# A separate body for experts with up to 32 rows, on four column groups of TensorE

## What is computed

```python
logits = hf @ router_w + router_b                    # (256, 32)
top_val, top_idx = lax.top_k(logits, 4)
top_w = jax.nn.softmax(top_val, axis=-1)
...
def expert_block(args):                              # x of one expert's rows
    xb, e = args
    g = xb @ w_gate[e] + b_gate[e]                   # w_gate, w_up, w_down: (1024, 1024)
    u = xb @ w_up[e] + b_up[e]
    g = jnp.minimum(g, SWIGLU_LIMIT)
    u = jnp.clip(u, -SWIGLU_LIMIT, SWIGLU_LIMIT)
    act = g * jax.nn.sigmoid(SWIGLU_ALPHA * g) * (u + 1.0)
    return act @ w_down[e] + b_down[e]
...
y = y.at[row_tok].add(yb * row_w[:, None])
```

## Time and profile before

| | us |
|---|---|
| median of 3 runs | 2553.96 |
| lowest, highest | 2553.76, 2555.77 |
| span of the profiled execution | 2552.7 |
| expert stage in it, first gate matmul to the end of the last combination | 442.1 to 1437.7 |
| experts 12 and 13, up to up | 831.00 to 860.41 |

### The profile page before, as it was taken

One profiled execution on the slowest core, in us unless ns is written; L12 is line 12 of the kernel. 1 busy time (PEld: TensorE's weight loads), 2 busy tenths in 40 slices (PEclk: granted clock), 3 DMA queues, 4 the chain that ended last, 5 costly groups with the idle time before them and its releaser, 6 DMA issues.

```text
span 2552.7 us, 24185 instructions
## 1 busy us (share of the span) xinstructions
PE 2212.0 (87%) x9951; PEld 1237.3 (48%) x9952; DVE 651.7 (26%) x997; ACT 357.1 (14%) x548; POOL 103.9 (4%) x116
## 2 busy tenths in 40 slices
PE   6977789998899999999999797799979686858997
PEld 2643346333333333333333384488548475837873
DVE  2747623110111111111111115100016465420000
ACT  1211012111111111111111212100012221211000
POOL 1000010000000000000000100200000031200000
PEclk9888889999999999999999898899979887988999
DMA  9561155998699999969999741343333200013330
GB/s 346 207 230 50 66 192 204 398 428 359 263 427 428 427 428 428 428 262 413 428 427 417 290 163 65 83 151 146 133 130 132 99 1 1 1 67 116 139 109 17
DMA packets 106791, 580.77 MB, mean 228 GB/s; under 512 B 6992, under 2 KB 8084, under 8 KB 81969
## 3 DMA queue, kind: packets, MB, share of 16 engines
q1 hardware_dynamic: 101008, 562.40, 55.1%
q0 software_dynamic: 5696, 17.18, 2.2%
HBM read 578.49 MB, written 1.07 MB: 227 GB/s over the span
## 4 chain that ended last, share of the span: by engine, by line
PE 67%; DMA 16%; DVE 11%; ACT 3%; issue 2%; SPq 0%; DVEq 0%; POOL 0%; ACTq 0%
DMA ring<-in_w_up 14%; PE ps L1199 14%; PE ps L1586 12%; PE ps L1597 6%; PE ps L604 6%; PE ps L612 5%; PE ps L1214 5%; PE ps L516 1%; PE ps L1931 1%; PE ps L1222 1%; PE ps L1937 1%; DMA ring<-in_ada_w 1%; PE ps L825 1%; PE ps L1941 1%; PE ps L793 1%
## 5 line engine op out<-in xcount | busy, mean ns | idle before, releaser
L1199 PE MATMUL ps<-ring,arena 128*64 128x512 f32 x1632 | 362.6, 598 | 29.5 <-DMA ring<-in_w_up 23.5
L1586 PE MATMUL ps<-arena,ring 128*128 128x256 f32 x1408 | 308.2, 382 | 1.5 <-ACT arena L581 1.5
L1586 PEld LDWEIGHTS ps<-arena,ring 128*128 128x128 f32 x1408 | 270.0, 192 | 39.6 <-ACT arena L581 2.3
L1214 PE MATMUL ps<-ring,arena 128*64 128x512 f32 x1088 | 240.9, 594 | 9.0 <-ACT arena L1161 9.0
L1199 PEld LDWEIGHTS ps<-ring,arena 128*64 128x64 f32 x1632 | 114.7, 138 | 271.7 <-issue 231.2
L1134 DVE TENSOR_SCALAR arena<-ps 128x512 f32<-128x512 f32 x34 | 23.5, 692 | 546.3 <-PE ps L1199 546.3
L1214 PEld LDWEIGHTS ps<-ring,arena 128*64 128x64 f32 x1088 | 88.3, 137 | 139.1 <-issue 138.3
L1597 PE MATMUL ps<-ring,arena 128*128 128x512 f32 x352 | 151.4, 592 | 0.0
L604 PE MATMUL ps<-arena,ring 128*128 128x256 f32 x672 | 149.1, 384 | 0.7 <-ACT arena L581 0.7
L604 PEld LDWEIGHTS ps<-arena,ring 128*128 128x128 f32 x672 | 129.1, 193 | 20.4 <-issue 1.5
L1199 PE MATMUL ps<-arena 128*64 128x512 f32 x544 | 124.5, 611 | 11.2 <-issue 11.2
(11 more groups left out here) (453 smaller groups left out, 2147.5 us busy)
## 6 DMA issues: line engine op xcount, KB each, us to landing
ring<-in_w_up SPq DMA_DIRECT2D x64, 2048.0 KB, 17.3
ring<-in_w_down SPq DMA_DIRECT2D x64, 2048.0 KB, 16.2
ring<-in_w_gate SPq DMA_DIRECT2D x32, 2048.0 KB, 15.9
arena<-in_w_gate SPq DMA_DIRECT2D x32, 2048.0 KB, 15.9
ring<-in_ffn_w_gate_up SPq DMA_DIRECT2D x22, 2048.0 KB, 7.9
ring<-in_ada_w SPq DMA_DIRECT2D x12, 2048.0 KB, 17.7
ring<-in_ffn_w_down SPq DMA_DIRECT2D x10, 2048.0 KB, 7.7
ring<-in_w_in SPq DMA_DIRECT2D x8, 2048.0 KB, 18.0
```

The source lines that it names most:

```text
L1199: m = pe.matmul(bank(b)[c * CAP:(c + 1) * CAP, :], xT[:, j * P + h * CAP:j * P + (h + 1) * CAP], w[h][:, j, c * 512:(c + 1) * 512], start= ...
L1214: m = pe.matmul(bank(b)[d * CAP:(d + 1) * CAP, :], actT[:, j * P + h * CAP:j * P + (h + 1) * CAP], down_w[h][:, j, d * 512:(d + 1) * 512], ...
L1586: m = pe.matmul(bank(b0 + g)[:, c * SEQ:(c + 1) * SEQ], w[:, k, (2 * g + c) * P:(2 * g + c + 1) * P], hT2[:, k, :], start=(k == 0), stop=( ...
```

## The change

Experts with up to 32 rows (`FEW`) take a body of their own, `few`, which lies in the loop ahead of `narrow`; each engine now has two branches in a body. On PE:

- gate and up are one product. Each step of the contraction has four matmuls of 32 array columns: gate's two halves and up's two halves, side by side in one bank. 32 matmuls in 8 steps. It starts when both gate and up are there, and `g_ps` and `u_ps` are both raised by its last step. The biases are four more matmuls behind the first step.
- gather, transposes of gathered rows, weights and hidden values follow, in another order than before.
- down has four groups too: two halves of the output by two halves of the contraction, 16 matmuls in 4 steps. The two contraction halves stay on different rows of PSUM; the combination adds them, because its matrix now holds each weight twice.

For that, DVE's `dve_choose` makes the combination matrix in three instructions for each of the two token tiles instead of one (in the first round of every expert, whatever its body), with two tables, `far` and `both`, made once ahead of the loop. `pe_open` moves in the narrow, wide and further bodies from ahead of the combination of the expert before to the start of its own expert. In the bodies for over 128 rows a branch is dropped. SP's code is not touched.

```diff
+FEW = CAP // 2
...
+            o(dve.tensor_scalar(far, bank(7)[:, 2 * E:3 * E], float(FEW), float(2 * SEQ), ALU.is_gt, ALU.mult))
+            o(dve.tensor_scalar(both, posm, float(FEW), None, ALU.add))
+            o(dve.tensor_tensor(both[:, :, 0:E], both[:, :, 0:E], rows_bc(far, TT), ALU.add))
             o(dve.tensor_copy(cnt, bank(7)[:, 2 * E:3 * E]), pos_ready)
...
-                m = dve.tensor_scalar(Pw[:, t, :], slot_iota(r, 2 * CAP), posm[:, t, bass.ds(e, 1)], wt[:, t, bass.ds(e, 1)],
-                                      ALU.is_equal, ALU.mult)
+                if r == 0:
+                    dve.tensor_scalar(Pm, slot_iota(0, 2 * CAP), posm[:, t, bass.ds(e, 1)], None, ALU.is_equal)
+                    dve.drain()
+                    dve.scalar_tensor_tensor(Pm, slot_iota(0, 2 * CAP), both[:, t, bass.ds(e, 1)], Pm, ALU.is_equal, ALU.add)
+                    dve.drain()
+                    m = dve.tensor_scalar(Pw[:, t, :], Pm, wt[:, t, bass.ds(e, 1)], None, ALU.mult)
...
         def pe_narrow(pe, e, odd, there):
             n = e + 1
+            pe.wait_ge(main.pwT_ready, n)
+            pe_open(pe, 0, odd, 0)
+            pe_open(pe, 1, odd, 1)
             pe.wait_ge(main.x_ready, n * 2)
...
-            pe.wait_ge(main.pwT_ready, n + 1)
-            pe_open(pe, 0, 1 - odd, 0)
-            pe_open(pe, 1, 1 - odd, 1)
             pe_combine(pe, main, n, PwT[odd])
+
+        def pe_few(pe, e, odd, there):
+            n = e + 1
+            pe.wait_ge(main.pwT_ready, n)
+            pe.wait_ge(main.x_ready, n * 2)
+            there(0)
+            there(1)
+            for h in range(2):
+                for j in range(4):
+                    for i, (w, done) in enumerate(((gate_w[odd], main.g_ps), (up_w, main.u_ps))):
+                        for c in range(2):
+                            m = pe.matmul(bank(0)[(2 * i + c) * FEW:(2 * i + c + 1) * FEW, :],
+                                          XT[:, j * P + h * CAP:j * P + h * CAP + FEW], w[h][:, j, c * 512:(c + 1) * 512],
+                                          start=((h, j) == (0, 0)), stop=((h, j) == (1, 3)), tile_position=(0, (2 * i + c) * FEW), skip_group_check=True)
+                        if (h, j) == (1, 3):
+                            m.then_inc(done, 1)
+                    if (h, j) == (0, 0):
+                        for i in range(2):
+                            for c in range(2):
+                                pe.matmul(bank(0)[(2 * i + c) * FEW:(2 * i + c + 1) * FEW, :], Ee[odd][i * E:(i + 1) * E, 0:FEW],
+                                          bgu[i * E:(i + 1) * E, c * 512:(c + 1) * 512], start=False, stop=False,
+                                          tile_position=(i * E, (2 * i + c) * FEW), skip_group_check=True)
+            pe_gather(pe, main, n + 1)
+            pe_gatherT(pe, main, n * 2 + 1)
+            pe.wait_ge(main.a_ready, n * 2)
+            pe_weights(pe, main, n + 1)
+            for j in range(4):
+                m = pe.transpose(bank(0)[:, j * CAP:(j + 1) * CAP], every4(act_[0:CAP, :], j), ident[0:CAP, 0:CAP])
+            m.then_inc(main.aT_ps, 1)
+            there(2)
+            pe.wait_ge(main.aT_ready, n)
+            for j in range(4):
+                for d in range(2):
+                    for h in range(2):
+                        g = 2 * d + h
+                        m = pe.matmul(bank(2)[g * FEW:(g + 1) * FEW, :], actT[:, j * CAP + h * FEW:j * CAP + (h + 1) * FEW],
+                                      down_w[h][:, j, d * 512:(d + 1) * 512], start=(j == 0), stop=(j == 3), tile_position=(0, g * FEW))
+            m.then_inc(main.d_ps, 1)
+            pe_combine(pe, main, n, PwT[odd])
...
         def pe_wide(pe, e, odd, x, there):
+            pe.wait_ge(main.pwT_ready, n)
+            pe_open(pe, 0, odd, 0)
+            pe_open(pe, 1, odd, 1)
...
                     n_e = eng.value_load(cnt[0:1, bass.ds(e, 1)], min_val=0, max_val=SEQ)
+                    eng.br_cond(n_e > FEW, f"many_{which}{odd}", f"few_{which}{odd}")
+                    nc.switch_bb(f"few_{which}{odd}", parent=fork)
+                    few(i, e, odd)
+                    eng.br(f"next_{which}{odd}")
+                    nc.switch_bb(f"many_{which}{odd}", parent=fork)
                     eng.br_cond(n_e > CAP, f"large_{which}{odd}", f"small_{which}{odd}")
```

More of the change, by code:

```diff
@@ L987, in block_kernel @@
         mk = ar3(13792, 64, TT)
+        far, both = ar(21504, E), ar3(21536, TT * (E + 1), TT)
+        Pm = ar(21632, P)
         wt, posm = ar3(13856, TT * (E + 1), TT), ar3(13924, TT * (E + 1), TT)
@@ new lines, in act_few @@
+        def act_few(act, e, odd):
+            n = e + 1
+            act.wait_ge(main.gm_ready, n)
+            act.activation(sg[0:CAP, :], gm[0:CAP, :], ACT.Sigmoid, scale=ALPHA).then_inc(main.sg_ready, 1)
+            act_gathered(act, main, n * 2 + 1)
+            act_gatheredT(act, main, n * 2 + 2, XT)
+            act_weights(act, main, n + 1, PwT[1 - odd])
+            act.wait_ge(main.aT_ps, n)
+            act.copy(actT[:, 0:4 * CAP], bank(0)[:, 0:4 * CAP]).then_inc(main.aT_ready, 1)
+            act_out(act, main, (main.d_ps, n))
@@ new lines, in dve_few @@
+        def dve_few(dve, e, odd):
+            n = e + 1
+            dve.wait_ge(main.pwT_ps, n)
+            dve_choose(dve, main, e + 1, 0, 1 - odd)
+            dve.wait_ge(main.u_ps, n)
+            dve.tensor_scalar(gm[0:CAP, :], bank(0)[0:CAP, :], LIMIT, None, ALU.min).then_inc(main.gm_ready, 1)
+            dve.tensor_scalar(um[0:CAP, :], bank(0)[CAP:2 * CAP, :], LIMIT, -LIMIT, ALU.min, ALU.max).then_inc(main.a_ready, 1)
+            dve.drain()
+            dve.scalar_tensor_tensor(um[0:CAP, :], um[0:CAP, :], 1.0, gm[0:CAP, :], ALU.add, ALU.mult)
+            dve.drain()
+            dve.wait_ge(main.sg_ready, n)
+            dve.tensor_tensor(act_[0:CAP, :], um[0:CAP, :], sg[0:CAP, :], ALU.mult).then_inc(main.a_ready, 1)
@@ L1321, in pe_further @@
             pe.wait_ge(main.x_ready, e * 2 + 2)
+            pe.wait_ge(main.pwT_ready, e + 1)
+            pe_open(pe, 0, odd, 0)
+            pe_open(pe, 1, odd, 1)
             pe_gather(pe, extra, x)
@@ L1349, in dve_further, with expert_rounds @@
             dve_glu(dve, extra, x, (extra.g_ps, x), (extra.u_ps, x))
-        def expert_rounds(eng, narrow, wide, further):
+        def expert_rounds(eng, few, narrow, wide, further):
             which = eng.engine.name
```

22 lines of the change are left out of this document (9 added, 13 removed).

## The result

The changed kernel takes 2638.6 us (median of 4, 2636.3 to 2643.2) against 2554.9 of the kernel before on the same chip (2553.8 to 2561.8): 1.033 times, interval 1.031 to 1.035. A second comparison gave 2644.8 against 2553.3, 1.036 (1.033 to 1.038). The direction was forecast, the size was not: about 84 us instead of 38.5, and above the upper end of the range, 2612. The profiled execution has a span of 2634.3 us, 81.6 more than before, and all of it lies in the expert stage, which now ends at 1520.9 instead of 1437.7.

A forecast was written before the change was run, and what follows sets the result against it. The weight stream's transfers were taken to bound the kernel. Gaps +41.0, small terms +3.3, +0.5, -0.8, +0.6 and the stage's end -6.1 gave +38.5 us: 2592.5 us, main range 2575 to 2610, with (a) 2558 to 2612.

The forecast's parts named there:

- The slack of 7.9 us: Weight queue in the full stream: a gate transfer may be issued 7.9 us later before the stream gets a gap.
- The eleven places of the gaps: Few experts whose gap counts in full: 1, 2, 12, 13, 15, 17, 18, 24, 25, 28, 29; +41 us in all.
- The end: End of the expert stage: T + 42.6 us, T being when expert 30's up has landed, instead of 48.7 behind it.
- Up of expert 31: End of the stage: its second half lands at T + 23 us, T being when expert 30's up has landed.
- Part 2: Few experts' joined products: idle PE lowers the clock, adding 2.2 us (1.4 to 2.7), so each gap is 3.7 us.
- the 1.5: Stream delay per few expert at full clock, in us, from gate issued 9.45 us later against the slack of 7.9.
- Part 5: Moved openings, DVE's choice, extra branches: no cost in the stream; narrow bodies at 28.8 us, still under 29.4.
- rival (c): PE's doubled loop code must be fetched again in each body: some +60 us more, 2652 us; chance 0.06.
- Part 4: End of the expert stage, experts 30 and 31: shorter by 6.1 us.
- Rival (b): PE is the limit where the chain names it, so faster: 2505 us, or 2549 in a milder form; chance 0.08.
- (d): Column groups from different buffers don't overlap: joined product takes 14 us instead of 7, 2670 us; chance 0.03.
- (a): Gaps without the clock: it stays at 1.00, so +12 us, 2566 us; chance 0.14.

The follow-up runs named there:

- parted_nowide: Changed kernel with gate and up computed apart again, in two groups each, and the wide body never taken: 2491.6 us.
- warm_split: Changed kernel, wide body never taken, with 16 unread filling matmuls between the waits for gate and up and 8 behind the combination of few bodies: 2544.4 us.
- never_few: Changed kernel with the few bodies in the loop but never taken, experts up to 64 rows running the narrow body: 2599.6 us.
- no_few: Changed kernel with the few bodies' code and branch removed from the loop, openings at the start and DVE's longer choice kept: 2557.2 us.
- tail_joined: Kernel before's loop with DVE's longer choice, last pair of experts taken out and given the change's own few body: 2554.3 us, 1.000 times the kernel before.
- parted: Changed kernel with gate and up computed apart again, each in two groups of 32 columns, the rest of the few body kept: 2585.7 us.
- swapped: Few bodies in the loop but never taken, with the odd wide body ahead of the even one in memory: 2596.0 us.

## Why the prediction was wrong in size

**Right.** The kernel is bound by the stream of weights, and its price is the time of issue: confirmed by parted_nowide. The joined product costs what one product did, 8.2 us with its biases at full clock (experts 0 and 31). The slack of 7.9 us: with the gate issue found at T + 11.8 it gives 1.25 + 11.8 - 7.9 = 5.1 (5.15), and the five gaps from expert 12 to 20 are 4.9 to 5.8; with the issue of warm_split at T + 8.4 it gives 1.8, measured 2.0. The eleven places of the gaps, none behind narrow bodies. The end: 43.4 us instead of 42.6. Up of expert 31, T + 24.1 instead of T + 23.

**Part 2, the clock's term, mis-sized.** The gap was to be 1.5 + 2.2 = 3.7. Over the nine gaps in the stream (experts 12 to 29) it is 5.1 in the mean: the product is 3.4 us longer than its 8.2 (2.7 to 4.0), and the other 1.6 to 2.0 are the later issue. So the 1.5 was near, and the 2.2 was the term that failed. I took the mean of three products behind idle times of 5.5 to 5.8 us (excess 1.4, 2.6, 2.7), and reckoned with 10 us of idle time ahead of each few body. The idle time is no guide to the excess:

| ahead of the product | idle, us | longer than 8.2 by |
|---|---|---|
| narrow, expert 12 | 5.3 | 3.4 |
| narrow, experts 15, 17, 24 | 7.0 to 7.1 | 3.7 to 4.0 |
| narrow, expert 28 | 8.1 | 2.7 |
| few, expert 29 | 10.5 | 2.8 |
| few, experts 13, 18, 25 | 11.8 to 12.1 | 3.2 to 3.5 |

At expert 12 the product stays at 0.50 for 6.7 us, with its biases at 1.86 us instead of 0.99, behind no more idle time than in the kernel before. What keeps the clock down longer here than in the earlier trace rows is not shown. The end of my range (3.4) was the better value, but no row of before said so. This step is 14 of the 45 us that are missing.

**Part 5 and rival (c), instruction fetch, put at nothing.** This is the larger miss, about 30 of the 45 us. I gave the longer loop no cost, and (c) 0.06 at +60 us, because the earlier trace rows shows no fetch in six turns of the loop. That was read correctly and is still so. But the rows speak of a loop that is left alone. The relevant rows were those of the returns: one stall of 5.71 at expert 7 in the earlier trace rows, none behind 21. I wrote down the branches out and back as given costs, and did not ask what a loop twice as long makes of the return. It makes 31 us more of stalls in the chain (48.2 instead of 17.0), and never_few against no_few shows 42 for the longer loop. The mechanism of (c) was real, its place was wrong: it acts not at each body but at the first turns of the loop behind a wide one, exactly where the stream is empty and PE leads, so that nothing hides it.

**Part 5, the openings.** Forecast at no cost for narrow bodies in the stream, and 0.5 - 0.8 + 0.6 elsewhere: no_few shows +5.4. A narrow body, forecast at 28.8 us and 28.5 in no_few, is under 29.4, but at the start and behind a wide one PE leads for four to six experts, and each pays the 0.75 us over the 27.77 of before.

**Part 4, right as a term of this kernel, wrong as a gain.** -5.4 in the changed kernel; by itself, in tail_joined, the end is 2.5 us shorter in the trace and nothing shows in the medians; a lower clock takes part of it.

**Rival (b)** is refuted by the sign and by parted (half of down for nothing), **(d)** by the product's 8.2 us, **(a)** by the clock rows.

**Slips of the sum.** 11 x 3.7 is 40.7, not 41, so that the terms give 38.2; and the pieces of a narrow body (7.0, 4.0, 7.0, 1.9) add up to 19.9, not 19.6. Neither matters beside the two misses.

## What to carry to other kernels

Before two operands' products are joined, ask which transfer the first of them releases: in a kernel bound by a stream, a product that starts when its own operand lands is worth more than one that is twice as short. Put a shorter body only where PE's work sets the end (here the last two experts), and look for what code in a loop costs when the loop is entered again after a far branch, and not at its steady turns alone. When a change moves idle time ahead of a product that others wait for, carry the clock's price as a range up to beyond the largest value in the trace: the mean of three rows was 1.2 us too low for each gap, and the length of the idle time did not order them.

## What the runs showed of the hardware

- Code that is never run cost 42 us (never_few against no_few), mostly through stalls of 10.5, 10.5 and 15.6 us after two excursions to far code; the order in memory of the far code did not matter (swapped, 2596.0 against 2599.6). One execution with as long a loop (parted) had no stall behind the first excursion.
- Behind 5.3 us without work PE ran at 0.50 for 6.7 us of a product; such a product was 2.7 to 4.0 us longer behind 5.3 to 12.1 us of idle time, in no order with it, and 1.4 to 2.7 us behind 5.5 to 5.8 us in the kernel before. Filling work brought the clock back to 1.00 and the product from 11.6 to 8.2 us.
- Four groups of 32 columns ran fully side by side in float32, with 512 columns (8.2 us with biases for 72 records) and with 256 (3.8 us for 64). The Trainium skill (TensorE: Matmul & The Clock Gate, Part 3) has 2.38 times for three column tiles; an estimate from it, 79% of the ideal, would make the product 8.7 us without its biases. The rows, with four tiles, show 7.2.
